# A ring of four expert matrices, a second expert fetched before the routing is known, and TensorE's expert program written out without a loop

## The reference

```python
def moe_ffn(u, w_router, b_router, w_gate, b_gate, w_up, b_up, w_down, b_down):
    logits = (xf @ w_router + b_router).astype(F32)
    top_val, top_idx = lax.top_k(logits, TOP_K)          # 4 of 32
    gates = jax.nn.softmax(top_val, axis=-1)
    ...
    def expert_rows(args):
        xblk, e = args
        gt = jnp.minimum(xblk @ w_gate[e] + b_gate[e], SWIGLU_LIMIT)
        up = jnp.clip(xblk @ w_up[e] + b_up[e], -SWIGLU_LIMIT, SWIGLU_LIMIT)
        hdn = (up + 1.0) * gt * jax.nn.sigmoid(gt * SWIGLU_ALPHA)
        return hdn @ w_down[e] + b_down[e]
```

## Time and profile before

| | us |
|---|---|
| median of 3 runs | 1269.01 (1265.29 to 1271.62) |
| the profiled execution, its own time | 1267.89 |
| its span, first to last instruction | 1266.1 |
| PE busy | 1171.0 (92%) |
| DVE busy | 487.8 (39%) |
| ACT busy | 196.0 (15%) |
| all DMA | 451.35 MB, mean 357 GB/s |
| granted PE clock, mean | 0.974 of full |

### The profile page before, as it was taken

How to read it: one execution, slowest core, us unless ns; L and a number is a source line. 1 busy time by engine, 2 the same in 40 slices (tenths; PEclk the granted TensorE clock), 3 DMA queues, 4 the chain that set the end, 5 groups by cost and what they waited for, 6 DMA issues and landing times.

```text
span 1266.1 us, 21176 instructions
## 1 busy us (share of the span) xinstructions
PE 1171.0 (92%) x8462; PEld 553.0 (44%) x8463; DVE 487.8 (39%) x1083; ACT 196.0 (15%) x432; POOL 5.4 (0%) x33
## 2 busy tenths in 40 slices
PE   8999989999899999999899999899999888979896
PEld 6888768874333333433333433333433333233233
DVE  2999997015332322232312233222232232323233
ACT  2144513021111111011101111100111111011012
POOL 0000000000000000000000000000000000000000
PEclk9999998999998999999989999999999899999898
DMA  9542338615999999899999999998999999999995
GB/s 394 226 170 88 121 148 313 272 44 193 396 428 424 429 427 424 338 430 429 429 428 386 358 430 429 429 429 353 396 430 429 429 429 427 430 429 428 428 431 215
DMA packets 36996, 451.35 MB, mean 357 GB/s; under 512 B 5112, under 2 KB 5656, under 8 KB 10080
## 3 DMA queue, kind: packets, MB, share of 16 engines
q1 hardware_dynamic: 35344, 449.02, 85.2%
q10 hardware_dynamic: 1616, 1.82, 0.4%
HBM read 443.57 MB, written 7.25 MB: 356 GB/s over the span
## 4 chain that ended last, share of the span: by engine, by line
PE 57%; DMA 28%; DVE 11%; issue 2%; DVEq 1%; ACT 0%; POOL 0%; SPq 0%; POOLq 0%; ACTq 0%
DMA ring<-in_w_experts 28%; PE ps L1482 23%; PE ps L1525 10%; DVE acts L734 5%; PE ps L1254 3%; PE ps L1459 3%; PE ps L1361 3%; PE ps L1418 2%; PE ps L1492 2%; PE ps L1534 2%; PE ps L1228 2%; PE ps L1472 1%; DVE acts L829 1%; PE ps L1352 1%; PE ps L1515 1%
## 5 line engine op out<-in xcount | busy, mean ns | idle before, releaser
L1482 PE MATMUL ps<-ring,extra 128*64 128x512 f32 x1824 | 418.4, 603 | 12.2 <-DMA ring<-in_w_experts 12.2
L1087 DVE TENSOR_TENSOR acts<-ps,acts 128x528 f32<-128x528 f32 x128 | 90.6, 708 | 393.1 <-PE ps L1492 199.5
L1525 PE MATMUL ps<-ring,extra 128*32 128x256 f32 x3072 | 207.2, 405 | 37.0 <-DMA ring<-in_w_experts 31.2
L1482 PEld LDWEIGHTS ps<-ring,extra 128*64 128x64 f32 x1824 | 123.0, 138 | 262.4 <-issue 233.5
L1525 PEld LDWEIGHTS ps<-ring,extra 128*32 128x32 f32 x3072 | 91.2, 114 | 142.6 <-issue 51.4
L734 DVE SCALAR_TENSOR_TENSOR acts<-acts,small 128x256 f32<-128x256 f32 x224 | 91.2, 474 | 1.1 <-ACT acts L461 1.1
L1254 PE MATMUL ps<-acts,ring 128*128 128x280 f32 (+1 forms) x320 | 75.3, 394 | 0.3 <-ACT ring L534 0.3
L1254 PEld LDWEIGHTS ps<-acts,ring 128*128 128x128 f32 x320 | 60.5, 190 | 14.2 <-issue 1.0
L1254 PE MATMUL ps<-acts,extra 128*128 128x280 f32 x256 | 61.3, 400 | 1.9 <-DVE acts L716 1.9
L1101 DVE TENSOR_SCALAR extra<-ps 128x512 f32<-128x512 f32 x32 | 22.0, 689 | 97.6 <-PE ps L1482 82.1
L1459 PE MATMUL ps<-acts 128*64 128x512 f32 (+1 forms) x228 | 57.3, 623 | 0.0
(11 more groups left out here) (299 smaller groups left out, 895.9 us busy)
## 6 DMA issues: line engine op xcount, KB each, us to landing
ring<-in_w_experts SPq DMA_DIRECT2D x192, 2048.0 KB, 20.5
ring<-in_w_in_t SPq DMA_DIRECT2D x5, 2048.0 KB, 20.9
extra<-in_w_in_t SPq DMA_DIRECT2D x4, 2048.0 KB, 11.0
extra<-in_w_out_t SPq DMA_DIRECT2D x4, 1024.0 KB, 5.9
ring<-in_w_out_t SPq DMA_DIRECT2D x4, 1024.0 KB, 6.0
ring<-in_state_t SPq DMA_DIRECT2D x8, 512.0 KB, 7.4
ring<-dtx_rows SPq DMA_DIRECT2D x8, 512.0 KB, 6.4
out_ssm_s_t<-ring SPq DMA_DIRECT2D x8, 512.0 KB, 5.4
```

Of the source, the lines that this page charges most:

```text
L1087: TT(both, ps[:, 6:8, 0:TN], both, ALU.add).then_inc(ev["acc_done"], 1)
L1482: hs.append(MM(dst, src[:, o:o + HALF], piece(p)[:, k, 512 * h_:512 * (h_ + 1)], start=(fresh and kk == 0), stop=(kk == KT - 1), skip_grou ...
L1525: hs.append(MM(dst, src[:, o:o + QUAR], piece(p)[:, k, 256 * q:256 * (q + 1)], start=(fresh and kk == 0), stop=(kk == KT - 1), skip_group_ ...
```

## The change

- **Ring.** `ring` grows to 16 pieces: four slots of one matrix (4 MB). Matrix m of position i lies in slot (3i + m) modulo 4. The 4 MB (32 KB per partition) come from `acts`, whose views are packed more tightly; some mixer buffers (`cbuf`, `csmp`, `csq`) move into the new slot, and the routing tables into `small`.
- **Expert 1 second.** It gets position 1 whatever its count (24 here), as a big expert. Its gate matrix is prefetched into the fourth slot during the sample states, its other four pairs are issued without waiting for `order_ready`. Positions 2 and 3 are now small experts; from 4 on big and small alternate. The big experts of rank 2 to 15 go by 6r modulo 28, so that the wide ones (now rank 2, 3, 4) stand at 12, 18 and 24.
- **PE's program.** All 32 positions are written out, without a loop; the widths are still chosen by branches. The four scatters of the former expert come together after the first gate piece, through banks 6/7 and 4/5 in turn, so that a scatter waits for the add two before it. In a small expert only the scatters stand twice, no longer the gate products. The sorting products of position 0 stand after its first gate piece and scatters, in bank 3.
- DVE, ACT and SP keep loops, now over positions 4 to 31 (SP: 2 to 31).

```diff
-        ring = sb("ring", NP * PIECE)
+        MAT = 4 * PIECE
+        NQ = 4
+        ring = sb("ring", NQ * MAT)
         extra = sb("extra", 4 * PIECE)
-        acts = sb("acts", 16400)
+        acts = sb("acts", 12064)
...
-        def piece(p):
-            return view(ring, p * PIECE, 2, D)
-
-        def pair_row(q):
-            return view(ring, 2 * q * PIECE, 2 * PIECE)
-
+        def matrix_at(i, m):
+
+            return (i * 3 + m) % NQ * MAT
+
+        def span(at, n):
+
+            return ring[:, at:at + n] if isinstance(at, int) else ring[:, bass.ds(at, n)]
+
+        def pair_row(i, q):
+            return span(matrix_at(i, q // 2) + (q % 2) * 2 * PIECE, 2 * PIECE)
+
+        BACK_BANK = (6, 4, 6, 4)
+        sorted_ps = ps[:, 3, 0:6 * NE]
         LAST_BANK = (6, 4, 2, 6)
...
-            def prefetch(q):
-                sp.dma_start(pair_row(q), expert_pair(0, q)).then_inc(landed[q], 16)
+            def prefetch(q, i=0):
+                sp.dma_start(pair_row(i, q), expert_pair(i, q)).then_inc(landed[i][q], 16)
 
...
+                if b == NB - NST_IN:
+                    sp.wait_ge(ev["var_mm"], 1)
+                    sp.wait_ge(ev["kept_out"], 64)
+                    prefetch(0, 1)
+                    prefetch(1, 1)
...
+            def stream(i, e, par, first=0):
+                for q in range(first, NP // 2):
+                    if q < 2:
+                        sp.wait_ge(ev["piece_used"], i * 8 - 16 + 6 + 2 * q)
+                    elif q < 4:
+                        sp.wait_ge(ev[("gate_half", "gate_used")[q - 2]], i)
+                    else:
+                        sp.wait_ge(ev["piece_used"], i * 8 - 8 + 2 * (q - 3))
+                    sp.dma_start(pair_row(i, q), expert_pair(e, q)).then_inc(landed[par][q], 16)
+
+            stream(1, 1, 1, 2)
             sp.wait_ge(ev["order_ready"], 1)
-            with sp.Fori(0, NE - 1) as i:
-                e = sp.value_load(order[0:1, bass.ds(i + 2, 1)], min_val=0, max_val=NE - 1)
-                for q in range(2):
-                    sp.wait_ge(ev[("gate_half", "gate_used")[q]], i + 1)
-                    sp.dma_start(pair_row(q), expert_pair(e, q)).then_inc(landed[q], 16)
-                for q in range(2, NP // 2):
-                    sp.wait_ge(ev["piece_used"], i * 8 + 2 * q - 2)
-                    sp.dma_start(pair_row(q), expert_pair(e, q)).then_inc(landed[q], 16)
+            with sp.Fori(0, NE // 2 - 1) as ii:
+                for par in range(2):
+                    e = sp.value_load(order[0:1, bass.ds(ii * 2 + 3 + par, 1)], min_val=0, max_val=NE - 1)
+                    stream(ii * 2 + 2 + par, e, par)
 
...
+            V.memset(krow[:, 1:2], 5.0e5)
...
-            TS(wrap_a, rank, 5.5, -16.0, ALU.is_gt, ALU.mult)
-            TS(wrap_b, rank, 10.5, -16.0, ALU.is_gt, ALU.mult)
+            TS(wrap_a, rank, 5.5, -28.0, ALU.is_gt, ALU.mult)
+            TS(wrap_b, rank, 9.5, -28.0, ALU.is_gt, ALU.mult)
+            TS(wrap_c, rank, 14.5, -28.0, ALU.is_gt, ALU.mult)
             TS(is_small, rank, NE - NSMALL - 0.5, None, ALU.is_gt)
-            TS(place, rank, -4.0, 33.0, ALU.mult, ALU.add)
-            v.drain()
-            STT(wrap_a, rank, 3.0, wrap_a, ALU.mult, ALU.add)
+            TS(fix1, rank, 1.0, -5.0, ALU.is_equal, ALU.mult)
+            TS(fix16, rank, 16.0, None, ALU.is_equal)
+            TS(place, rank, -4.0, 53.0, ALU.mult, ALU.add)
+            v.drain()
+            STT(wrap_a, rank, 6.0, wrap_a, ALU.mult, ALU.add)
+            TT(wrap_b, wrap_b, wrap_c, ALU.add)
             TT(place, place, is_small, ALU.mult)
+            TT(fix16, fix16, fix1, ALU.add)
             TS(krow2, eye4, is_small, None, ALU.mult)
             v.drain()
             TT(wrap_a, wrap_a, wrap_b, ALU.add)
-            v.drain()
-            STT(place, wrap_a, 2.0, place, ALU.mult, ALU.add)
+            TT(place, place, fix16, ALU.add)
+            v.drain()
+            TT(place, wrap_a, place, ALU.add)
             v.drain()
             TS(pick[:, 2:NE + 1], iota_f[:, 1:NE], place, None, ALU.is_equal)
             V.memset(slotp_s, -FAR)
...
+            def big_expert(i, k, small_next):
+                add_back(i * 4)
+                if isinstance(i, int) and i == 0:
+                    take_order()
...
-            def piece_products(p, b, src, bank, fresh, i16):
-                pe.wait_ge(landed[p // 2], i16)
+            def weights_of(i, par, n16):
+
+                return [matrix_at(i, m) for m in range(3)], landed[par], n16
+
+            def weight(w, p, k, c, n):
+
+                return span(w[0][p // 4] + (p % 4) * PIECE + k * D + c, n)
+
+            def piece_products(p, b, src, bank, fresh, w):
+                pe.wait_ge(w[1][p // 2], w[2])
...
-                if m:
-                    pe.wait_ge(ev["acc_done"], n4 + m)
+                if m > 1:
+                    pe.wait_ge(ev["acc_done"], n4 + m - 1)
                 for b in range(n):
                     for h_ in range(2):
                         rows = slice(HALF * h_, HALF * (h_ + 1))
-                        h = MM(ps[:, 6 + h_, 0:TN], ys[rows, 512 * b + P * m:512 * b + P * (m + 1)], Pm[rows, b, :],
+                        h = MM(ps[:, BACK_BANK[m] + h_, 0:TN], ys[rows, 512 * b + P * m:512 * b + P * (m + 1)], Pm[rows, b, :],
                                start=(b == 0), stop=(b == n - 1))
                 h.then_inc(ev["sc_done"], 1)
...
+            def small_back(i):
+                former_ready(i)
+                for m in range(4):
+                    scatter_s(m, i * 4)
+
+            def big_back(i, former):
+                former_ready(i)
+
+                def back(n):
+                    for m in range(4):
+                        scatter(n, m, i * 4)
+
+                by_width(former, back)
+
...
                 pe.wait_ge(ev["oh_ready"], i + 1)
                 pe.wait_ge(ev["xt_ready"], i * 2 + 2)
-
-                def former_rows(n, p):
-                    if p == 0:
-                        former_ready(i)
-                    scatter(n, p, i * 4)
-
-                by_width(former, lambda n: gate_s(i * 16 + 16, lambda p: former_rows(n, p)))
-                up_s(i * 16 + 16)
+                gate_s(w, back)
+                up_s(w)
                 pe.wait_ge(ev["s_ready"], i + 2)
-                by_width(following, gather)
...
-            big_expert(0, first, find_order)
-            small_expert(1, first, count_of(3))
-            with pe.Fori(0, NE // 2 - 1) as ii:
-                count, following = count_of(ii * 2 + 3), count_of(ii * 2 + 5)
-                big_expert(ii * 2 + 2, count)
-                small_expert(ii * 2 + 3, count, following)
+                if following is None:
+                    pe.wait_ge(ev["xg_out"], i * 2 + 4)
+                    turn_s(xg, 2, ev["xt_done"])
+                else:
+                    by_width(following, turn_next(i))
+                down_s(i * 2, w)
+
+            def first_back():
+                small_back(0)
+                find_order()
+
+            big_expert(0, weights_of(0, 0, 16), first, first_back, second, True)
+            big_expert(1, weights_of(1, 1, 16), second, lambda: big_back(1, first), None)
+            small_expert(2, weights_of(2, 0, 32), lambda: big_back(2, second), None)
+            small_expert(3, weights_of(3, 1, 32), lambda: small_back(3), count_of(5))
+            now = count_of(5)
+            for i in range(4, NE, 2):
+                coming = count_of(i + 3)
+                big_expert(i, weights_of(i, 0, i // 2 * 16 + 16), now, lambda: small_back(i), None)
+                small_expert(i + 1, weights_of(i + 1, 1, i // 2 * 16 + 16), lambda: big_back(i + 1, now), coming)
+                now = coming
             pe.wait_ge(ev["o_tab"], 1)
             n_over = pe.value_load(otab[0:1, OVER:OVER + 1], min_val=0, max_val=OVER)
             pe.wait_ge(ev["xt_ready"], NE * 2 + 2)
@@ -1774,12 +1875,13 @@
                         pe.wait_ge(ev["xt_ready"], j * 2 + 2 * (NE + 2))
                         bias(0, 64)
                         bias(2, 96)
-                        gate_of(2, j * 16 + 16 * (NE + 1), lambda n, p: None)
-                        up_of(2, j * 16 + 16 * (NE + 1))
+                        w = [0, MAT, 2 * MAT], landed[0], j * 16 + 8 * NE + 16
```

More of the change, by code:

```diff
@@ L174, in build @@
         kcol, rank, place, wrap_a, wrap_b, is_small, cntcol = (view(acts, 1672 + i, 1) for i in range(7))
+        wrap_c, fix1, fix16 = (view(acts, 2016 + i, 1) for i in range(3))
         slotp_s = view(acts, 1680, 3, NE + 2)
@@ new lines, in build, with rt @@
+        Pm = view(acts, 5984, 2, TN)
+        gp = view(acts, 6512, TN)
+        eq = view(acts, 7712, 3, TOPK, NE)
+        yo = view(acts, 7712, KT, TN)
+        fsq = view(acts, 2240, KT, TN)
+        frstd = view(acts, 5600, TN)
+        ro = [route0]
+        def rt(*dims):
+            n = 1
+            for d in dims:
+                n *= d
+            v = view(small, ro[0], *dims)
```

(16 more changed lines are left out.)

309 lines of the change are left out of this document (161 added, 148 removed).

## The result

The changed kernel takes 1258.0 us (median of 8 runs, 1254.3 to 1263.4), the kernel before 1268.95 (8 runs on the same chip): a ratio of 0.9917, 95% interval 0.9896 to 0.9939. It is 0.8% or 11 us faster, where the forecast had 25 us and 1244. The profiled execution took 1256.9 us.

The account below looks back on a forecast made before the run. From 308 us on the DMA, at 429 GB/s, was taken to bound the kernel, not PE. Against the profiled 1267.9 us, -9.8 - 23.5 + 4 + 3 + 1 = -25.3 gave 1242.6, as a median 1244 us; range 1233 to 1262.

Parts of the forecast that it names:

- PE's code streamed: +3: PE's written-out program: some 90 code packets, 1.5 MB, take 3.4 us of the DMA, 3 more than before.
- PE's stalls on code: +1: PE waiting for code behind jumps: 1 us more, bounds 0 to 26, as the code that stalled most is gone.
- None was fetched again in the loop: PE's old loop: its body stayed resident, with 24 code packets by 450 us and 26 in all.
- Fourth slot and order: Ring two pairs longer and wide experts later: all three DMA dips close, -23.5 us, bounds -15 to -25.
- rival B: Expert stage: the dips stay, each back by half or more, for about 1258 us; chance 0.10.
- Two pairs early: -9.8: Expert 1's two gate pairs, issued behind the last state load, leave the expert stage's transfer: -9.8 us.
- expert 1 big: +4: Start of the expert stage: a big expert frees its pairs more slowly while the ring is full, +4 us, bounds 0 to 8.
- Order no longer awaited: 0: First refill of the ring: it waited for PE, not for the order, so no gain or loss, bounds -1 to +2.
- Back products: 0: Scatters through banks 4 to 7: waits for adds, 2.9 us instead of 2.6, offset by the loop's head going; 0.
- Rival A: PE stalls on its own code, new for each pair: 3.6 us a pair gives 1269 us; chance 0.19.
- the rate near 429 with nothing under 410: Sign in the DMA's slices after 320 us: GB/s stays near 429, no value under 410.
- wide experts 176 apart: Sign in the expert stage: wide experts follow each other in about 176 us.

Follow-up runs that it names:

- lean: The changed kernel with code for wide experts only at positions 0, 1, 12, 18, 24 and 30; 1252.5 us, ratio 0.9871.
- dead2: The changed kernel plus 64 never executed matmuls in a branch at the end of each big expert from position 4 on; 1266.5 us, ratio 0.9984.
- e4: The kernel before with only the wide experts moved to positions 12, 18 and 24; 1271.4 us, ratio 1.0001.
- e5: The changed kernel with the wide experts back at positions 6, 12 and 18; 1257.8 us, ratio 0.9912.
- e2_late: The changed kernel with expert 1's two gate pairs issued at the start of the stream instead of ahead of expert 0's; 1262.8 us, ratio 0.9934.
- lean_back2: lean with the back products in two halves, behind gate pieces 0 and 1; 1250.6 us, ratio 0.9860.
- nw_straight: The kernel before with PE's loop written out straight and the wide branch never taken; 1261.5 us, ratio 0.9936.
- e1_loop2: The changed kernel with PE's positions 4 to 31 as a loop of seven turns over four positions; 1294.2 us, ratio 1.0180.
- lean_loop: lean_back2 with wide experts at 6, 12 and 18 and PE's positions 20 to 31 as a loop of three turns; 1244.7 us, ratio 0.9820.
- nw_after: The changed kernel with its wide branch in the program but never taken; 1253.0 us, ratio 0.9878.

## Why the prediction was wrong

- **"PE's code streamed: +3" is the step that failed**, and "PE's stalls on code: +1" with it. I counted bytes at the full rate (1.5 MB, 3.4 us), as if all sixteen engines shared them. Each packet held up one of eight engines by 1.54 us, which for the 77 packets more of the changed kernel is an estimate of 77 / 8 x 1.54 = 14.8 us. Measured, straight code costs 14.8 us on the old ring and 14.7 with no wide experts: 7 us of steady rate, 2.5 to 6 at the end, 3 to 7 in slow stretches. With 14.8 in place of 4 the forecast would have been 1255; 1258 were measured. That lies within the stated range, 1233 to 1262, but above the forecast's own 1250.
- "None was fetched again in the loop" was right, and the number of packets (100 said, 103 found). The Trainium skill ("Runtime: NRT & Kernel Launch", Instruction fetch mechanics) has a first-in first-out buffer refilled in blocks of 16 KiB and no instruction cache, and says that kernels prefer full unrolling where possible. The runs say otherwise: bodies of 6.3 and 6.6 pages were not refetched, one of 11.5 was, and unrolling cost 14.8 us. The size that it gives for PE, 128 KiB or eight such pages, lies between.
- **Fourth slot and order: -23.5 said, -14.4 found.** 9.1 us of dips stayed (windows at 660, 840 and 1020). That is less than the half that rival B needed, so the time that B names, 1258, was met by luck: the cause is another. With a smaller program (lean) 5.3 stay, with code that is jumped over (dead2) 24.3: so the dips grow with the code again. I take PE's "issue" idle (13 us) for the way, as part of it falls into wide pairs, where PE has nothing to spare; that is argued and not measured. "With the later wide experts" was no part of it (e4, e5). How much would stay with no code at all wasn't tried: the new ring can't be run from a one-pair loop, as its slots differ from pair to pair.
- **Two pairs early: -9.8, expert 1 big: +4.** In sum -5.8, and e2_late has -4.7 in its trace. The net held, within what one trace of each can tell, though the loss comes from the full ring and not from expert 1's size: without the early pairs the start loses 1.8 us.
- **Order no longer awaited: 0** held: the first refill came at 311.65 when PE had used the gate pair. That is 3.6 us later than before, but 2.6 of them the mixer was late.
- **Back products: 0** missed 10.6 us of PE's waits for adds. Without them (lean_back2) the account is 1.0 us shorter, and the time can't be told from lean's.
- **Rival A** was right in what it blamed and wrong in the way. Stalls come to 13 us in 16 pairs, 0.8 a pair and not 3.6; nw_straight shows that the price is paid by the DMA even where PE has time. I weighed code only as a burden on PE because a pair's 90 KB looked small beside 25 MB of weights.
- Of the signs named ahead, the packets (103) and the stalls under 2 us a pair came true; the rate near 429 with nothing under 410 (426, and 371 at the lowest), wide experts 176 apart (181) and weights 25 us earlier (1249.4 to 1237.8, so 11.6) did not. The first of these, 3 GB/s in every undisturbed slice, is the one that points at the cause.

## What to carry to other kernels

Where the DMA sets the end, a program written out straight is traffic: it cost 0.17 us a page here (14.8 us for 86 packets), also for code that is only jumped over. Such a cost isn't bytes over the total rate: it is set by the slowest of the engines that share a transfer, so look at how far apart the completions of one DMA lie. Unroll only as far as the new freedom needs, cut what a position can't execute, and turn the rest into loops short enough to stay resident (6.6 pages did, 11.5 didn't). Together with split scatters this took the kernel from 1258 to 1245; of the single steps only the cut (lean) is clear of noise in time. A prefetch into a ring that is full at the start gives back part of what it saves, because the DMA then waits for the first release.

## What the runs showed of the hardware

- A code packet of 16 KB took 1.04 us, a weight packet of 16 KB 0.62 (means of the changed kernel's trace); with some 100 of them in 926 us the DMA's undisturbed rate fell from 429 to 425 or 426 GB/s, and with none of them in a stretch it was 428 again.
- The code packets held up eight of the sixteen DMA engines and never the others: within one weight DMA of nw_straight eight completions keep their distances for 270 us, the other eight fall behind by 1.54 us of one engine for each code packet.
- In e1_loop2, where the loop body was fetched in every turn, each jump back left PE idle for 7.1 to 7.6 us. "Issue" idle of PE was up to 2.5 us at once in the changed kernel, and up to 4.3 in dead2, with its jumps over a whole page.
- A loop body of 6.3 or 6.6 pages (101 or 106 KB, before and lean_loop) was fetched once; one of 11.5 pages (e1_loop2) in every turn.
- With streamed code the sixteen completions of the last weight DMA lay 4.5 to 17.3 us apart (lean, nw_after); in the four kernels with the old loop, 1.8 to 3.0.
